# GpSimd's low parts in quarters, and other places in the order for the convolution, the memory rows, the first scan and the last attention steps

## The reference

```python
x = x + 0.5 * swiglu(rmsnorm(x, ffn1_norm), ffn1_w_gu, ffn1_w_down)     # hidden width 2816
h = rmsnorm(x, mix_norm); p = h @ w_in            # columns: q | f | i | g (512 each), gb | gc | u (512 each)
f = lb + (1 - lb) * sigmoid(fz); k = 1 - f        # 4 heads of 128: gated linear recurrence in chunks of 64
o_hg = rmsnorm(hgrn2_chunkwise(silu(q), log f, k, i), hg_norm) * silu(g)
o_cv = rmsnorm(gb * causal_dwconv(gc * u, conv_w), conv_norm)           # 3 taps, 512 channels
x = x + concat(o_hg, o_cv) @ w_out
x = x + cross_attention(rmsnorm(x, xa_norm), rmsnorm(mem, mem_norm))    # 4 heads of 256, 256 memory rows
x = x + 0.5 * swiglu(rmsnorm(x, ffn2_norm), ffn2_w_gu, ffn2_w_down)
out = rmsnorm(x, final_norm)
```

## Time and profile before

| | |
|---|---|
| runs of the kernel | 1162.81, 1164.76, 1164.62 us (median 1164.62) |
| profiled execution | 1163.28 us |
| its span, first to last instruction | 1161.5 us |
| PE busy | 1141.4 us (98%) |
| DVE, ACT, POOL busy | 465.8, 432.2, 548.4 us |
| stages on PE, from to (us) | first FFN 1 to 374, mixing 374 to 577, w_out 577 to 627, keys 627 to 653, attention 653 to 744, wo 744 to 791, second FFN 791 to 1155 |

### The profile page before, as it was taken

The page is one execution under the profiler, slowest core; times in us unless marked ns, Lnnn a source line. Parts: engine busy times, 40 slices in busy tenths (PEclk is TensorE's granted clock), DMA queues, the critical chain, the costliest instruction groups (busy, mean ns, idle before and its releaser), DMA issues.

```text
span 1161.5 us, 14979 instructions
## 1 busy us (share of the span) xinstructions
PE 1141.4 (98%) x5382; PEld 951.1 (82%) x5382; DVE 465.8 (40%) x662; ACT 432.2 (37%) x586; POOL 548.4 (47%) x404
## 2 busy tenths in 40 slices
PE   9999999999999999999999999999999999999997
PEld 7888888888887888887878888788888888888886
DVE  6432322322223667877567223454322322321112
ACT  6423223222223545553246543344222222222222
POOL 0745445455554433333326873155545445455550
PEclk9999999999999999999999999999999999999999
DMA  7332232233223222111222542122332232233312
GB/s 230 127 108 90 90 108 90 90 109 109 99 100 108 73 73 74 64 66 64 79 91 91 182 163 73 37 74 93 107 108 90 90 108 90 90 109 109 107 57 73
DMA packets 36965, 113.10 MB, mean 97 GB/s; under 512 B 3776, under 2 KB 10048, under 8 KB 36800
## 3 DMA queue, kind: packets, MB, share of 16 engines
q1 hardware_dynamic: 35728, 111.00, 28.7%
q10 hardware_dynamic: 1200, 1.57, 0.4%
HBM read 110.47 MB, written 2.10 MB: 97 GB/s over the span
## 4 chain that ended last, share of the span: by engine, by line
issue 39%; PE 33%; POOL 26%; POOLq 0%; DVE 0%; ACT 0%; DVEq 0%
POOL wl L349 26%; PE bank L1007 11%; PE bank L1008 11%; PE bank L1009 11%; POOLq L347 0%; POOLq L345 0%; DVE x L994 0%; PE n_bank L1050 0%; PE o_bank L1155 0%; DVEq L100 0%; ACT rstd L612 0%; DVE x L987 0%; PE n_bank L1153 0%; PE n_bank L1155 0%; ACT rstd L613 0%
## 5 line engine op out<-in xcount | busy, mean ns | idle before, releaser
L349 POOL TENSOR_TENSOR wl<-raw,wh 128x512 fp32r<-128x512 f32 x400 | 548.2, 1394 | 587.5 <-ACT wh L360 320.4
L1007 PE MATMUL bank<-xh,wh 128*128 128x512 f32 x936 | 369.6, 395 | 0.0
L1009 PE MATMUL bank<-xh,wl 128*128 128x512 f32 x936 | 364.8, 390 | 0.0
L1008 PE MATMUL bank<-xl,wh 128*128 128x512 f32 x936 | 364.7, 390 | 0.0
L373 ACT ACTIVATE wh<-raw 128x1024 fp32r<-128x1024 f32 x104 | 110.3, 1061 | 391.9 <-DVE ubuf L700 218.6
L1007 PEld LDWEIGHTS bank<-xh,wh 128*128 128x128 f32 x936 | 176.0, 188 | 38.4 <-issue 1.9
L1008 PEld LDWEIGHTS bank<-xl,wh 128*128 128x128 f32 x936 | 176.1, 188 | 37.5 <-issue 1.7
L1009 PEld LDWEIGHTS bank<-xh,wl 128*128 128x128 f32 x936 | 175.9, 188 | 37.0
L360 ACT ACTIVATE wh<-raw 128x1024 fp32r<-128x1024 f32 x96 | 101.1, 1053 | 131.2 <-PE bank L1009 130.5
L1007 PE MATMUL bank<-hid_h,wh 128*128 128x512 f32 (+1 forms) x374 | 141.0, 377 | 0.0
L1009 PE MATMUL bank<-hid_h,wl 128*128 128x512 f32 (+1 forms) x374 | 140.8, 377 | 0.0
(11 more groups left out here) (216 smaller groups left out, 1097.2 us busy)
## 6 DMA issues: line engine op xcount, KB each, us to landing
raw<-w_all SPq DMA_DIRECT2D x200, 512.0 KB, 3.3
x<-x_t SPq DMA_DIRECT2D x8, 256.0 KB, 6.1
out_t<-x SPq DMA_DIRECT2D x8, 256.0 KB, 2.5
raw<-w_all SPq DMA_DIRECT2D x6, 256.0 KB, 6.2
memf<-mem_t ACTq DMA_DIRECT2D x1, 1024.0 KB, 4.9
raw<-w_all ACTq DMA_DIRECT2D x2, 256.0 KB, 4.3
gbuf<-masks_d SPq DMA_DIRECT2D x1, 256.0 KB, 6.2
ident<-ident_d SPq DMA_DIRECT2D x1, 64.0 KB, 5.8
```

The lines of the kernel that those rows point to most:

```text
L349: ins = nc.gpsimd.tensor_tensor(wl[:, c, half], raw[:, c, half], wh[:, c, half].bitcast(f32), SUB)
L1007: nc.tensor.matmul(out_, a[0], b_[0], start=first, stop=False)
L1008: nc.tensor.matmul(out_, a[0], b_[1], start=False, stop=False)
L1009: return nc.tensor.matmul(out_, a[1], b_[0], start=False, stop=last)
```

## The change

**GpSimd.** The low part of a unit is made in four operations of 128 x 256 instead of two of 128 x 512. The signal still comes after the last.

**Convolution.** In `MIX_SLOTS` B goes behind C and u of its channel group. C's factor is multiplied by the norm twice (a further operation after the steps of its slot), u is read from PSUM straight into the product with it, the taps follow behind the steps of u's slot, and the norm is multiplied in there; B's unit, one to four slots later, is then multiplied by the finished taps straight from PSUM. The count of large DVE operations of a channel group stays 8.

**First scan.** Head 0's step A moves from slot 1 to slot 0, and with it the first two differences and exponentials. ACT's extra table load ahead of `mixcol` goes.

**Convolution's sum.** TensorE's sum of squares moves from chunk 2 of `together` to chunk 0. `together` starts with one chunk for the four groups instead of two and ends with three instead of two.

**Memory.** `memf`, `mh`, `ml` get another place in SBUF, their load goes out at slot 26, squares and sums (into an own buffer `msq`) stand ahead of w_out's group 0, TensorE's sum behind `together`, and the norm and the split go two chunks at a time to groups 2 to 5.

**Attention.** q 7 goes ahead of O 1. T 2 and S 3 move behind wo's chunk 0, O 2 behind chunk 1; T 3 stays behind chunk 2, O 3 goes from chunk 4 to chunk 3.

The diff, cut to its core:

```diff
@@ the lists
-             ("f", 1), ("q", 1), ("g", 0), ("B", 0), ("C", 0), ("f", 2),
...
+             ("f", 1), ("q", 1), ("g", 0), ("C", 0), ("u", 0), ("f", 2),
+             ("B", 0), ("q", 2), ("f", 3), ("g", 1), ("C", 1), ("u", 1),
+             ("q", 3), ("g", 2), ("g", 3), ("B", 1), ("C", 2), ("u", 2), ("B", 2), ("C", 3), ("u", 3), ("B", 3)]
-            ("q", 4), ("S", 1), ("q", 5), ("q", 6), ("T", 1), ("S", 2), ("O", 1), ("q", 7), ("T", 2), ("S", 3), ("O", 2)]
+            ("q", 4), ("S", 1), ("q", 5), ("q", 6), ("T", 1), ("S", 2), ("q", 7), ("O", 1), ("T", 2), ("S", 3), ("O", 2)]
+XA_OWN = XA_ORDER.index(("T", 2))
+          if HEAD_START[h] + r - (h == 0 and r == 0) == at] for at in range(len(MIX_SLOTS))]
@@ gpsimd
-                    for half in (slice(0, UNIT // 2), slice(UNIT // 2, UNIT)):
-                        ins = nc.gpsimd.tensor_tensor(wl[:, c, half], raw[:, c, half], wh[:, c, half].bitcast(f32), SUB)
+                    for k in range(0, KC, 2):
+                        two = slice(128 * k, 128 * k + 256)
+                        ins = nc.gpsimd.tensor_tensor(wl[:, c, two], raw[:, c, two], wh[:, c, two].bitcast(f32), SUB)
@@ scalar
-                if name != "ffn1":
+                if name not in ("ffn1", "mixcol"):
                     act.preload_act_table_set("natural_log_exp_and_others")
...
+                if at == len(MIX_SLOTS) - 2:
+                    act.wait_ge(cat_lo, HEADS)
+                    act.dma_start(memf[:, :, :], mem_t).then_inc(mem_loaded, 16)
+                if kind == "B":
+                    act.wait_ge(group_read, SLOT_GROUP[at] + 5)
                     square(convO[:, c, :], Q_CONV + c)
@@ vector
+                    if h == 0:
+                        differences(h, 0)
+                        differences(h, 1)
...
+                elif kind == "B":
                     dve.wait_ge(unit_used, U_MIX + at + 1)
+                    V_.tensor_tensor(convO[:, c, :], src, convV, MULT).then_inc(group_read, 1)
...
-                    V_.tensor_tensor(convU[:, 2:], src, rstd[:, :], MULT).then_inc(group_read, 1)
+                    V_.tensor_tensor(convU[:, 2:], src, convC[:, :], MULT).then_inc(group_read, 1)
...
+                if kind == "C":
+                    dve.wait_ge(group_read, g + 5)
+                    link(V_.tensor_tensor(convC[:, :], convC[:, :], rstd[:, :], MULT))
...
-                    V_.tensor_tensor(convO[:, c, :], convV, convB[:, :], MULT).then_inc(conv_new, 1)
+                    link(V_.tensor_tensor(convV, convV, rstd[:, :], MULT))
+                if kind == "B":
                     add_squares(Q_CONV + c)
@@ tensor
-                for k in range(2, KC - 2):
+                for k in range(KC - 3):
...
-            together(U_WOUT, G_WOUT, {2: lambda: sum_squares("conv", Q_CONV + CC)}, 0)
+            together(U_WOUT, G_WOUT, {0: lambda: sum_squares("conv", Q_CONV + CC)}, 0)
+            pe.wait_ge(msq_added, KC + 1)
+            n_wait("mem")
+            nc.tensor.matmul(n_bank[:, 0:M], ones[:, :], rstd[:, M:2 * M], start=True, stop=True).then_inc(n_done, 1)
...
-            together(U_WO, G_WO, {2: lambda: xa_step("T", 3), 4: lambda: xa_step("O", 3)}, KC)
+            together(U_WO, G_WO, {0: xa_steps(("T", 2), ("S", 3)), 1: xa_steps(("O", 2)),
+                                  2: xa_steps(("T", 3)), 3: xa_steps(("O", 3))}, KC)
```

More of the change, by code:

```diff
@@ L157, in block_kernel @@
         xa_mem = ExitStack()
[L158 to L163, removed]
         kv_mem = ExitStack()
@@ L494, in _, with decays @@
             ffn("ffn1", 0)
+            def decays(h, a):
+                for l in (2 * a, 2 * a + 1):
+                    act.wait_ge(diff_ready, DIFFS * h + l + 1)
+                    nc.scalar.activation(X[:, l % 2, :], X[:, l % 2, :], ACT.Exp).then_inc(exp_ready, 1)
             def step(kind, h, a):
@@ L505, in step @@
                     nc.scalar.activation(f, f, ACT.Identity, bias=one, scale=-1.0).then_inc(k_ready, 1)
[L506 to L509, removed]
+                    if h == 0:
+                        decays(h, 0)
+                if kind == "L" and (h, a) != (0, 0):
+                    decays(h, a)
                 if kind == "K":
@@ L546, in _ @@
                 nc.scalar.activation(cat_h[:, HEADS + c, :], convO[:, c, :], ACT.Copy).then_inc(cat_hi, 1)
-            act.wait_ge(cat_lo, KC)
-            act.dma_start(memf[:, :, :], mem_t).then_inc(mem_loaded, 16)
-            for m in range(KC):
[L551 to L555, removed]
+            act.wait_ge(mem_loaded, 16)
+            for k in range(KC):
+                if k >= 2:
+                    act.wait_ge(msq_added, k)
+                nc.scalar.activation(msq[:, k % 2, :], memf[:, k, :], ACT.Square).then_inc(msq_ready, 1)
+            for m in range(KC):
                 ahead(U_WOUT + m)
                 if m == 1:
[L558 to L562, removed]
+                    inverse_root("mem", rstd[:, 0:M], n_bank[:, 0:M], D)
                 new_x(2, m, Q_X2)
+                for k in range(2 * (m - 2), 2 * (m - 1)) if 2 <= m < 6 else ():
+                    act.wait_ge(mem_norm, k + 1)
+                    nc.scalar.activation(mh[:, k, :], memf[:, k, :], ACT.Copy).then_inc(mem_hi, 1)
             for g in range(KC):
@@ L810, in step @@
                         dve.wait_ge(silu_done, SN["q", h] + 1)
-                    differences(h, 2 * a)
-                    differences(h, 2 * a + 1)
+                    if (h, a) != (0, 0):
+                        differences(h, 2 * a)
+                        differences(h, 2 * a + 1)
                     if a > 0:
@@ L1261, in part @@
                                    (cat_h[:, k, :], cat_l[:, k, :]), k == 0, k == KC - 1)
-                pe.wait_ge(cat_lo, ready + 2)
-                for c in range(4):
-                    pe.wait_ge(lo_ready, u0 + c + 1)
-                    pe.wait_ge(group_read, g0 + c + 1)
-                    part(c, 0)
-                    part(c, 1)
-                for k in range(2, KC - 2):
+                for k in range(KC - 3):
                     pe.wait_ge(cat_lo, ready + k + 1)
                     for c in range(4):
+                        if k == 0:
+                            pe.wait_ge(lo_ready, u0 + c + 1)
+                            pe.wait_ge(group_read, g0 + c + 1)
                         part(c, k)
```

61 lines of the change are left out of this document (30 added, 31 removed), and 2 rows, old and new, of the table MIX_SLOTS.

## The result

The changed kernel takes 1151.41 us in the median of four runs (1150.43 to 1152.45), beside 1163.71 (1161.43 to 1164.76) for the kernel before on the same chip: a ratio of 0.9897, interval 0.9877 to 0.9918. It is faster by 1.03%; 1149.0 was forecast, with 1146.5 to 1156 as the range. Two runs at a much lower granted clock (1921.66 us of the kernel before, 5209.6 of the kernel with the memory rows back) are left out of all that follows. The profiled execution took 1150.43, its span is 1148.6. Three views of it, with the rows that answer to the earlier trace rows.

A forecast was written before the change was run, and what follows sets the result against it. PE was taken as the bound, busy 1141.4 of 1161.5 us. Removing 12.8 us of waits and 3.4 of clock loss, less 1.7 of new waits, takes 1163.28 to 1148.8, said as 1149; range 1146.5 to 1156.

The forecast's parts named there:

- S, cat_l, and qhl and pTl of the attention: PE's waits of 0.9, 0.9, 1.3 and 0.5 us for these values, all expected to go.
- Head 0's wait for X: Mixing part: the earlier scan removes 1.3 + 0.16 us, against 0.4 of a new wait.
- Head 3's kdT: Mixing part: moving the convolution to slot 17 removes a wait of 1.6 us and the clock's 1.7.
- three waits for wl: Low-part waits of 1.8, 0.4 and 0.2 us, with the clock's 1.7, to go under the memory part.
- the part on memory and `together`: w_out and keys: moved memory work and a longer `together` tail remove all waits there, with the clock's fall.
- the prediction's own sign against itself: Wrong if a wait over 1 us with a clock fall is left in the mixing part.
- First unit: Launch start: with quarters the first unit is ready at 30.53, wanted at 30.66, so 0.06 us of wait.
- q's bank: Head 0, mixing part: TensorE newly waits 0.4 us for DVE to empty the bank.
- That moves give nothing in the mixing part: Rival, 1 in 10: mixing waits turn up one step later; only w_out and attention gain, 1155, to 1162.
- GpSimd becomes the bound: Rival, 4 in 100: a quarter costs what a half does, so the kernel is slower, 1179 us.
- nothing new shows: Rival, 5 in 100: the new waits all fail to show and small gaps go, 1147 us or less.
- Some waits come back: Rival, 2 in 10: mixing-part waits and one lower clock return, 1153.6 us, range 1151.5 to 1156.

The follow-up runs named there:

- the memory rows back: Changed kernel with the memory rows' load, squares, sum, norm and split in their old places, the new `together` kept: 1152.76 us, ratio 0.9909.
- quarters alone: Kernel before with only GpSimd's two halves per unit replaced by four quarters: 1162.13 us, ratio 0.9985.
- the late fourth group: Changed kernel with the fourth group of `together` begun behind chunk 1 of the other three, in both output projections: 1146.34 us, ratio 0.9862.
- halves: Changed kernel with GpSimd's two operations of 512 columns instead of four quarters: 1152.87 us, ratio 0.9924.
- scan back: Changed kernel with head 0's step A at slot 1 again: 1154.72 us, ratio 0.9925.
- attention back: Changed kernel with the attention's order as before, wo keeping its one-chunk start and three-chunk end: 1155.59 us, ratio 0.993.

## Why the prediction was right, and where not

**The bound and the waits removed: right.** All twelve waits went, and both falls of the clock; S, cat_l, and qhl and pTl of the attention, came back when their part was undone. The parts were not as separate as I had them, though. Head 0's wait for X I gave to the scan alone; it needs the quarters as well. Head 3's kdT and its 1.7 of clock I gave to the convolution; quarters alone take 1.0 of the 1.6 and the whole fall. And for **Memory** I gave three waits for wl and 1.7 of clock to the memory rows' move; undone alone, the move costs 2.2 us, and the long wait and the fall go with quarters alone. I had priced the quarters' help at head 1's wait only.

**The step that failed is in the part on memory and `together`**, in what it leaves out: under *Attention* I worked out that "chunk 0 wants the low part of wo's fourth unit, whose slot is q 7's" and took 0.5 for it, but didn't ask the same of w_out's fourth unit, whose slot is that of B 3. There nothing like O 1 lies between, so 2.04 us of cover, where the kernel before had two chunks for each of the three groups, 4.08, stand against 1.06 + 3.23. Cost 4.3 us, the clock's 1.7 in it; the late fourth group gave back 4.1 from lowest to lowest run, 5.1 by the medians.

**The start offset it.** I made the sum against a profiled execution whose first matmuls were slow, and took this as part of the kernel. The one after had not: 1.9 us. Without it the profiled execution would have read about 1152.3. So the forecast was met to 1.4 us in part by luck: two errors, and 0.9 more gained in the attention than the forecast had, partly cancel; that a wait over 1 us with a fall of the clock would be left was the prediction's own sign against itself, and it stands just behind the mixing part, at w_out.

**The terms of the new waits** were 1.7 in all. First unit: 0.47 + 0.16 = 0.63 for 0.06; that stretch lost 0.36 net. I had priced a quarter at 0.68 from a memset's 0.10; it takes 0.739 in the middle and 0.716 at least, so what an operation costs beside its columns is 2 x 0.716 - 1.261 = 0.17 us. A unit takes 2.9 us and not 2.73. The estimate of 0.72 and 2.89 that stood beside it, from the Trainium skill (GPSIMD Engine Reference, "Performance versus the Vector engine"), was the better one. q's bank: 0.26 for 0.4; the scan ended at 381.91, which is the forecast 383.45 less the 1.55 by which this kernel is ahead there (372.30 for 373.85). Head 1's kd: 0.2 + 0.16 for 0.3. S and the convolution's sum: nothing, for 0.2 each. With the late fourth group the sum waits 0.54 (0.70 with the record's end), but there it comes 0.68 sooner, behind three groups; so at its own place, behind four, it is just in time even without the wait at w_out. wo: 0.54 + 0.16 for 0.5.

**DVE beside GpSimd: right.** A difference takes 0.96 beside a quarter, where it took 1.51 beside a half and 0.41 alone, under the bound of 1.1. The Trainium skill (SBUF — State Buffer, "Who interferes with whom") says of VectorE's modes with two ports that whoever issues first gets the shared pair for the whole instruction, and of an instruction with two SBUF inputs, as here, that it contends with GpSimd's reads. The trace fits the same rule for the latter: the stretching, 0.55 and 1.10, halves with the instruction.

**Attention: 2.63 gained for 1.9.** The waits account for 1.7 (2.4 removed, 0.70 new). Of the other 0.9, 0.6 is in the 96 matmuls of the values (`mh`, `ml`), each 512 columns: they start mostly 0.231 to 0.236 us apart in the kernel before and with quarters alone, and 0.227 in the changed kernel and in every version of it. With the memory steps back it is 0.227 too; `mh` and `ml` have the new place in SBUF there. That the place is the cause is likely and not shown. The prediction has no term for it. The rest, 0.3, stays open.

**The rivals.** That moves give nothing in the mixing part, that GpSimd becomes the bound and that nothing new shows all fell. "Some waits come back" gives the nearest picture (one wait and one fall of the clock more), though at another place and not by its bounds. (Of its bounds "1, 0.9 and 0.7 above" the 0.9 stands nowhere above; for the states it had taken 0.7, which makes 1.7 more and not 1.9. In the case of GpSimd as the bound, down units that go from 5.0 to 5.5 lose 0.5 each and not 0.3, 24 us and not 14.)

## What to carry to other kernels

When a step is priced at one place of a schedule, look for every other call of the same code: here the same function ran twice, and only one of its two heads was worked out. In a ring of buffers the question for each early reader is how much work lies between the release of its slot and its turn, against the chain that refills it. When a part is undone alone, what comes back is only what no other part covers: the quarters' worth at kdT and at the keys shows when they stand alone in the kernel before, and not when they are taken out of the changed one. And compare two kernels at landmarks stage by stage before crediting a difference to the change; 1.9 of these 12.9 us were the launch's start.

## What the runs showed of the hardware

The spacing of the first matmuls, 0.23 to 0.25 us or 0.43 to 0.46, follows the matmuls of ones ahead of them: with four all five runs took about the longer time, with ten (0.46 and 0.76 us idle in the two profiled executions) none of eight, with eight some. The length of the idle time doesn't decide: behind 0.80 us both occur, and behind 1.47 it was the short spacing. The windows' granted clock reads 1.00 in either case.

Later in the run the length of an idle time alone does not decide. The clock fell behind waits of 1.09 (halves, 452.61), 1.20 (scan back, 393.75), 1.6 and 1.76, 2.48 and 3.2 us, each time by some 1.7 us or more; it stayed at 1.00 behind 1.33 (halves, at 393.14, the same place as the 1.20), 2.0 (attention back), 2.2 (halves, w_out) and each wait of 1.2 to 1.3 with quarters alone. What else decides stays open. For a sum: a wait of 1 us and more may cost its length, or 1.7 us on top.

GpSimd's difference has a part of about 0.17 us that does not shrink with its columns, and VectorE's time beside it follows the length of GpSimd's instruction.
